# Value slabs ahead of query and key slabs at the head of a fused two-block kernel

## The reference

```python
h = rmsnorm(x, norm_mix)                 # x: 512 tokens x 1024
p = h @ w_in                             # retention: q, k, v, g of 512 columns each, then 1824 for RWKV-7
q, k = rope(q, positions), rope(k, positions) * 64 ** -0.5
s = (q_i . k_j) * gamma_h ** (i - j)     # i >= j, for each head h
y = s @ v                                # computed here over all 512 tokens at once
```

## Time and profile before

| | us |
|---|---|
| median of three runs | 1325.1 |
| lowest and highest | 1322.62, 1326.82 |
| the profiled execution's own time | 1322.79 |
| its span, first to last instruction | 1320.9 |
| mean granted TensorE clock in it | 0.989 |

### The profile page before, as it was taken

One profiled execution on the slowest core, in us unless ns is written; L12 is line 12 of the kernel. 1 busy time (PEld: TensorE's weight loads), 2 busy tenths in 40 slices (PEclk: granted clock), 3 DMA queues, 4 the chain that ended last, 5 costly groups with the idle time before them and its releaser, 6 DMA issues.

```text
span 1320.9 us, 20739 instructions
## 1 busy us (share of the span) xinstructions
PE 1262.7 (96%) x8308; PEld 1003.9 (76%) x8308; DVE 708.3 (54%) x827; ACT 542.7 (41%) x730; POOL 533.6 (40%) x245
## 2 busy tenths in 40 slices
PE   5999999888899999999999999999999999999995
PEld 3777757677787877788888888888776777777873
DVE  8888756757568532336224143144477755442833
ACT  5332253244343443543222132235342469885342
POOL 4442222710157732364444444446433322223453
PEclk9999999989999999999999999999999999999998
DMA  6571111110054221223222222222422321112221
GB/s 226 156 227 64 64 48 59 54 35 4 4 179 156 96 80 48 64 83 99 102 99 97 96 96 96 96 96 97 152 80 80 114 70 65 64 65 67 99 90 64
DMA packets 35098, 119.91 MB, mean 91 GB/s; under 512 B 4544, under 2 KB 4672, under 8 KB 34624
## 3 DMA queue, kind: packets, MB, share of 16 engines
q1 hardware_dynamic: 29808, 105.78, 23.7%
q10 hardware_dynamic: 5200, 12.85, 3.1%
HBM read 111.01 MB, written 2.10 MB: 86 GB/s over the span
## 4 chain that ended last, share of the span: by engine, by line
PE 79%; DVE 13%; ACT 4%; issue 2%; ACTq 1%; DMA 1%; POOL 0%; DVEq 0%; SPq 0%
PE banks L1381 20%; PE banks L1383 20%; PE banks L1382 20%; DVE y_mid L829 2%; PE banks L1402 1%; PE banks L1403 1%; PE banks L1404 1%; DVE tmp L829 1%; PE banks L1844 1%; PE banks L1860 1%; PE banks L1949 1%; DVE a_lo L837 1%; DVE qk L829 1%; PE banks L1934 1%; DVE x_res L837 1%
## 5 line engine op out<-in xcount | busy, mean ns | idle before, releaser
L338 POOL TENSOR_TENSOR w_lo<-w_raw,w_hi 128x1024 fp32r<-128x1024 f32 x145 | 353.7, 2440 | 537.7 <-ACT w_hi L401 537.4
L401 ACT ACTIVATE w_hi<-w_raw 128x1024 fp32r<-128x1024 f32 x145 | 153.8, 1061 | 333.1 <-PE banks L1383 213.2
L1381 PE MATMUL banks<-a_hi,w_hi 128*128 128x512 f32 x584 | 235.3, 403 | 14.2 <-DVE a_lo L837 12.2
L1383 PE MATMUL banks<-a_hi,w_lo 128*128 128x512 f32 x616 | 241.0, 391 | 0.0
L1382 PE MATMUL banks<-a_lo,w_hi 128*128 128x512 f32 x584 | 228.6, 391 | 0.0
L1383 PE MATMUL banks<-b_hi,w_lo 128*128 128x512 f32 x384 | 149.5, 389 | 0.0
L1381 PEld LDWEIGHTS banks<-a_hi,w_hi 128*128 128x128 f32 x584 | 110.0, 188 | 48.9 <-issue 16.9
L1383 PEld LDWEIGHTS banks<-a_hi,w_lo 128*128 128x128 f32 x616 | 116.2, 189 | 24.9
L829 DVE TENSOR_TENSOR x_res<-banks,x_res 128x512 f32<-128x512 f32 x56 | 38.7, 691 | 178.7 <-PE banks L1383 178.5
L338 POOL TENSOR_TENSOR w_lo<-w_raw,w_hi_mlp 128x1024 fp32r<-128x1024 f32 x36 | 87.2, 2423 | 106.4 <-ACT w_hi_mlp L401 106.4
L1382 PEld LDWEIGHTS banks<-a_lo,w_hi 128*128 128x128 f32 x584 | 110.4, 189 | 21.6 <-issue 0.7
(11 more groups left out here) (369 smaller groups left out, 2381.9 us busy)
## 6 DMA issues: line engine op xcount, KB each, us to landing
w_raw<-in_weights SPq DMA_DIRECT2D x189, 512.0 KB, 3.2
x_in<-in_x SPq DMA_DIRECT2D x4, 512.0 KB, 6.4
rot<-qk ACTq DMA_DIRECT2D x32, 64.0 KB, 2.0
decay<-in_decay ACTq DMA_DIRECT2D x1, 2048.0 KB, 9.7
x_res<-in_x ACTq DMA_DIRECT2D x4, 512.0 KB, 5.6
out_fm<-x_res SPq DMA_DIRECT2D x8, 256.0 KB, 2.1
consts<-in_consts SPq DMA_DIRECT2D x1, 1209.0 KB, 12.1
q_twice<-q_twice ACTq DMA_DIRECT2D x8, 128.0 KB, 3.2
```

The costliest lines, as they stand in the source:

```text
L338: nc.gpsimd.tensor_tensor(o, a, b, op).then_inc(S(name), 1)
L401: return nc.scalar.activation(o, a, f, **kw)
L1381: mm(o, high[:, w], hi[:, kc, :], start=kc == first, stop=False)
L1383: done = mm(o, w_lo[:, s % 4, w], hi[:, kc, :], start=False, stop=kc == last)
```

## The change

- Value slabs are 0 to 3; query and key slabs are 4 to 11, in the order query tile 0, key tile 0, query tile 1, key tile 1 and so on (`head_tile`). The weight layout follows.
- Value slab s starts with `a_lo` of its two x tiles. It is summed into banks 2 to 5; the values are scaled by VectorE in the second round, behind the rope of the first tile.
- ScalarE squares all eight x tiles, after the splits of slabs 0, 1 and 2; VectorE sums them; one matmul (two passes) with ones follows slab 2. GpSimd makes no squares.
- The slab 1 split comes after the fourth `a_hi`; SP loads weight slab 1 ahead of x tiles 4 to 7.
- ScalarE issues the loads of `w0` and `decay` behind the sum of squares, before the root; earlier they were issued at slab 8.
- The angle's last three VectorE operations come ahead of the reciprocal, and the cosine right behind it.
- Slab 12 follows the last key slab at once, so `rope(7)` and the `ret_lo` of the last three tiles come behind the masks of heads 0, 1 and 2. A pair of heads waits only for its own two tiles (`q_stacked0` to `q_stacked3`).
- `rot` moves from the place of `s_ret` to that of `kr`.

```diff
-S_RQ, S_RK, S_RV = 0, 4, 8
+S_RV, S_QK = 0, 4
-S_RET = S_RV + 4
+S_RET = S_QK + 8
+        def qk_taken(i):
+            return i + 1 if i < 2 else S_QK + i + 1
+        def head_tile(i):
+            return i // 2 + NF * (i % 2)
...
-                if s == 0:
-                    for i in range(4):
-                        load_x(i)
+                if s < 2:
+                    load_x(2 * s)
+                    load_x(2 * s + 1)
...
             for kc in range(KC):
                 x_hi(kc)
-            split_hi(1)
-            for kc in range(N_POOL_SQ, KC):
+                if kc == 3:
+                    split_hi(1)
+            split_hi(2)
+            for kc in range(KC):
                 x_squares(kc)
...
-                split_hi(s + 2)
+                if s > 0:
+                    split_hi(s + 2)
+                if s == 2:
+                    act.wait_ge(S("ssq_done"), 1)
+                    act.dma_start(w0[:], ins["w0"]).then_inc(S("decay_loaded"), 16)
+                    act.dma_start(decay[:], ins["decay"]).then_inc(S("decay_loaded"), 16)
+                    actv(rstd[:], psum[7][:], sqrt, bias=C("eps6"), scale=1.0 / DM).then_inc(A("rms_ready"), 1)
...
+                    if i == 1:
                         dve.wait_ge(S("column_done"), 1)
+                        cp(r_tok[:], psum[6][:, 0:8]).then_inc(D("column_ready"), 1)
+                        for t in range(TT):
+                            ts(v_ret[:, t, :], psum[2 + t][:], r_tok[:, 2 * t:2 * t + 1], None, ALU.mult).then_inc(D("tile_taken"), 1)
...
                 if S_RET <= s < S_RET + RH:
                     masked_scores(s - S_RET)
+                if s == S_WA:
+                    rope(7)
+                if S_WA <= s < S_WA + 3:
+                    ret_lo(s - S_WA + 5)
...
+                if s == 2:
+                    pe.wait_ge(S("x_sq_sum"), KC - 1)
+                    mm(psum[7][:], C("ones"), sq_in[:, 0, :], start=True, stop=True).then_inc(S("ssq_done"), 1)
+                if s == S_QK:
+                    pe.wait_ge(S("rstd_ready"), 1)
                     for t in range(TT):
+                        last = mm(psum[6][:, 2 * t:2 * t + 2], rstd[0:1, t * P:(t + 1) * P], C("ones", 0, 2)[0:1, :],
...
+                    if h % 2 == 0:
+                        pe.wait_ge(S("q_lo_ready"), 2 * h + 4)
+                        pe.wait_ge(S(f"q_stacked{h // 2}"), 4 * 16)
                     if h == 0:
-                        pe.wait_ge(S("q_lo_ready"), 16)
-                        pe.wait_ge(S("q_stacked"), 16 * 16)
                         pe.wait_ge(S("tile_taken"), S_RET)
+                        pe.wait_ge(S("column_ready"), 1)
```

More of the change, by code:

```diff
@@ L443, in exps, with swap_halves, ret_hi @@
                 actv(e_exc[:, f, :], be[:], exp).then_inc(A("exps_ready"), 1)
[L445 to L449, removed]
+            def swap_halves(i):
+                j = head_tile(i)
+                act.wait_ge(S("tile_taken"), qk_taken(i))
+                if i >= 2:
+                    act.wait_ge(S("rope_done"), i - 1)
                 for r in range(0, P, HD // 2):
                     o = r ^ (HD // 2)
[L452 removed]
+                    act.dma_start(rot[o:o + HD // 2, i % 2, :], qk[r:r + HD // 2, j, :]).then_inc(S(f"rot_loaded{i % 2}"), 16)
             def ret_part(j, k):
                 return q_twice[k][:, j, :] if j < NF else k_stack[k][:, j - NF, :]
[L458 to L459 removed]
+            def ret_hi(i):
+                j = head_tile(i)
+                act.wait_ge(S("rope_done"), i + 1)
                 for k in range(2):
@@ L470, in ret_stack @@
                     src = ret_part(j, k)[r] if j < NF else qk_lo[r, j, :]
-                    act.dma_start(ret_part(j, k)[other].bitcast(F32), src.bitcast(F32)).then_inc(S("q_stacked"), 16)
+                    act.dma_start(ret_part(j, k)[other].bitcast(F32), src.bitcast(F32)).then_inc(S(f"q_stacked{i // 2}"), 16)
             def silu(f):
@@ L485, in _ @@
                     actv(trig[:, 1, :], trig[:, 0, :], ACT.Sin, scale=0.5).then_inc(A("sines_ready"), 1)
[L486 to L494, removed]
+                i = s - S_QK
+                if 0 <= i < 8:
+                    swap_halves(i)
+                if 3 <= i < 11:
+                    ret_hi(i - 3)
+                if 4 <= i < 12:
+                    ret_stack(i - 4)
                 if s > S_RG:
@@ L872, in _ @@
                 x_lo(kc)
-            for kc in range(N_POOL_SQ + 1, KC):
+            for kc in range(1, KC):
                 x_square_sum(kc)
@@ L946, in _ @@
             mixed = [(low, 0), (low, 1), (low, 2)] + [(d, f) for d in (kk, rx, vx) for f in range(NF)]
[L947 to L953, removed]
+            for s in range(S_QK, S_MK):
                 dve.wait_ge(S("slab_done"), s + 1)
                 bank = psum[s % 2]
[L956 to L971, removed]
@@ L972, in _ @@
+                i = s - S_QK
+                if i < 8:
+                    tt(qk[:, head_tile(i), :], bank[:], rstd[:], ALU.mult).then_inc(D("tile_taken"), 1)
+                    if i >= 1:
+                        rope(i - 1)
+                    if i >= 3:
+                        ret_lo(i - 3)
+                    if i == 1:
                         dve.wait_ge(S("column_done"), 1)
[L973 to L976, removed]
+                        cp(r_tok[:], psum[6][:, 0:8]).then_inc(D("column_ready"), 1)
+                        for t in range(TT):
+                            ts(v_ret[:, t, :], psum[2 + t][:], r_tok[:, 2 * t:2 * t + 1], None, ALU.mult).then_inc(D("tile_taken"), 1)
@@ L1361, in _ @@
             mm = nc.tensor.matmul
-            wide_slabs = set(range(S_RV, S_WA)) | set(range(S_MV, S_WOUT)) | set(range(S_VIN, S_V2))
+            wide_slabs = set(range(S_RV, S_QK)) | set(range(S_MV, S_WOUT)) | set(range(S_VIN, S_V2))
             def begin(s):
@@ L1370, in begin @@
                 if before >= 0:
-                    pe.wait_ge(S("tile_taken"), before + 1)
+                    pe.wait_ge(S("tile_taken"), qk_taken(before - S_QK))
             def part(s, hi, lo, kcs, ready=None, k=0, at=0, first=0, last=KC - 1):
@@ L1396, in wide @@
                 for i, kc in enumerate(kcs):
+                    if ready:
+                        pe.wait_ge(S(ready), kc + 1)
                     for t in range(hi.shape[2] // P):
@@ L1469, in _ @@
             for s in range(S_MK):
-                if S_RV <= s < S_WA:
-                    if s == S_RV:
-                        pe.wait_ge(S("column_ready"), 1)
+                if s < S_QK:
                     i = s - S_RV
-                    wide(s, a_hi, a_lo, (2 * i, 2 * i + 1), (4, 5, 6, 7))
+                    wide(s, a_hi, a_lo, (2 * i, 2 * i + 1), (2, 3, 4, 5), "a_lo_ready")
                 else:
[L1476 to L1483, removed]
+                    slab(s, a_hi, a_lo)
+                if s == 2:
[3 more added lines that the diff above has]
+                    pe.wait_ge(S("rstd_ready"), 1)
                     for t in range(TT):
-                        last = mm(psum[5][:, 2 * t:2 * t + 2], rstd[0:1, t * P:(t + 1) * P], C("ones", 0, 2)[0:1, :],
+                        last = mm(psum[6][:, 2 * t:2 * t + 2], rstd[0:1, t * P:(t + 1) * P], C("ones", 0, 2)[0:1, :],
                                   start=True, stop=True)
@@ L2089, in lay_out @@
     rw = 2048
-    s = slabs(w_in[:, 0:1024]) + wide(w_in[:, 1024:1536])
+    s = wide(w_in[:, 1024:1536]) + slabs(w_in[:, 0:1024].reshape(DM, 2, NF, P).transpose(0, 2, 1, 3).reshape(DM, 1024))
     s += slabs(w_in[:, rw + 1536:rw + 1792]) + slabs(np.concatenate([w_in[:, rw + 1792:], pad], axis=1))
```

49 lines of the change are left out of this document (22 added, 27 removed).

## The result

The changed kernel takes 1327.56 us, the median of 20 runs (1323.28 to 1328.99); the kernel before, run beside it, 1325.24 (20 runs, 1320.73 to 1326.82). The ratio is 1.0016 with a 95% interval of 1.0008 to 1.0023: some 2 us slower, which is within the 0.3% that was called no change. The forecast was 1325.6 us, with a range of 1318.5 to 1329.5 that holds the result. The profiled execution took 1325.93 us, with a span of 1324.1 and a mean granted clock of 0.991.

A forecast was written before the change was run, and what follows sets the result against it. TensorE, busy 96% of the span, was taken as the bound. 6.9 gained, 4.9 lost waiting and 2.5 lost to the clock gave -0.5 us: forecast median 1325.6 us, range 1318.5 to 1329.5.

The forecast's parts named there:

- gain of 6.9 us: Up to the end of slab 12: 6.9 - 1.1 + 0.5 + 0.6 = 6.9 us gained.
- wait of 4.9: Behind slab 12: VectorE's backlog makes the first mask late, a loss of 4.9 us, bounds 4.2 and 5.9.
- clock loss of 2.5: Behind the wait for the first mask: TensorE's clock falls to 1.2 GHz, loss 2.5 us, bounds 0 and 2.9.
- the 4 to 6.5: Sign that the forecast is right: TensorE waits 4 to 6.5 us for `s_ret` near 94 to 100 us.
- First stretch: Value slabs in front: slab 1 starts at 17.7 us in place of 24.6, gain 6.9 us.
- waiting for the squares: After slab 2: the matmuls of the squares wait 0.5 us, part of a cost of 1.1 us.
- rival 3: Norm's chain late: TensorE waits 2 to 4 us before slab 5; time 1327.6 to 1329.6 us; chance 0.15.
- that is absorbed by the fifth round: Query and key rounds: four value tiles add 3.1 us of VectorE to the second round, absorbed by the fifth.
- Second hold: Behind slab 12: GpSimd's subtraction can hold VectorE's copy of `spread_r`, which then takes 1.7 us more.
- rival 2: Clock stays up: idle under 4.3 us with the copy first, 2.7 us gained, 1322.4 us; chance 0.15.
- Rival 1: No VectorE backlog: the mask is in time, no clock falls, 1318.2 to 1320.2 us; chance 0.25.
- carried along: Past 200 us: the change edits only one semaphore's count, so a time won earlier stays won.

The follow-up runs named there:

- e3_v_first: Changed kernel with the four value tiles scaled in the first query round, not the second; ratio 0.9994 to the kernel before.
- e1_again: Changed kernel run again with no edit; ratio 1.0014 to the kernel before.
- e4_act_order: Changed kernel with ScalarE's copies of a round put ahead of that round's rotation transfers; ratio 1.0016 to the kernel before.
- e2_fill: Changed kernel with dummy matmuls, nine ahead of slab 11 and twelve ahead of the scores of head 1; ratio 1.0020 to the kernel before.
- e5_clock: e3_v_first with 26 dummy matmuls in its only wait, ahead of the scores of head 1; ratio 0.9987 to the kernel before.
- e10_decay_late: Changed kernel with the loads of w0 and decay issued at slab 8 again; ratio 1.0014 to the kernel before.
- e6_spread_late: e3_v_first with VectorE's copy of spread_r moved three slabs later; ratio 0.9974 to the kernel before.
- e7_mask_first: e3_v_first with the spread_r copy three slabs later and each mask right behind shift, ahead of the mix's other operations; ratio 0.9965 to the kernel before.

## Why the prediction was right

**The sum held, in part by luck.** It had a gain of 6.9 us, a wait of 4.9 and a clock loss of 2.5: half a microsecond later. The mark is 0.55 us later. The kinds of loss were right, a late first mask and a clock that falls behind it. But four terms were off, and their errors cancelled: 1.6 us more was won up to slab 5, 2.6 us of waits came before slab 12 where the sum had a gain of 0.6, the wait for `s_ret` was 3.5 us, below the 4 to 6.5 that the prediction named as its sign, and the clock cost 0.7 us more.

**First stretch: right.** Up to slab 5 the sum was 6.9 - 1.1 + 0.5 = 6.3 us; measured 7.9. The clock rose 2.8 us sooner than in the profile of before, which is 1.4 of it. e3_v_first, with a rise at 14.8, starts slab 5 at 41.90: 6.8 us ahead. Of the 0.5 us of waiting for the squares 0.3 came: the last matmul of slab 2 starts at 27.30, the sums end at 27.78 and are used at 27.83. The norm's chain (rival 3) was in time with 2.6 us to spare: the reciprocal ends at 37.20, slab 4 at 39.8.

**The step that failed: "that is absorbed by the fifth round".** I put the value tiles into the second round at no cost beyond VectorE's time. But the third round's tile then comes 3 us late, its rotation issues with it (55.83), and VectorE stands idle for 3.92 us until they land. A subtraction held for 2.0 us follows (65.31). The tile of slab 8 starts 6.1 us after its slab ends (62.85), not about 2.5. So 0.4, 0.7 and 2.7 us of TensorE's waits and a first fall of the clock came before slabs 9 to 11, where I had 0.6 us, and the wait for `s_ret` was 3.5 us, below my 4.9. e3_v_first shows it: with the values one round earlier these three waits are gone and the one behind slab 12 is 6.4 us. The first mask starts at 98.82 us in after and at 96.88 in e3_v_first, with its copy held for 2 us: the step mostly moved where TensorE pays.

**Second hold: it comes in some profiles and not in others.** The copy of `spread_r` escaped in after by 0.6 us, and also in e1_again and e4_act_order (0.69 us each). It was held in e2_fill, e3_v_first, e5_clock and e10_decay_late (2.66 to 2.73 us). Moving it in e6_spread_late won 2.8 us of waiting: the whole held copy, 2.66 us, and not only my 1.7 for the hold.

**The clock: right in kind, mis-sized.** Falls came as forecast behind the long waits, and also behind one of 2.70 us; rival 2 is refuted. One costs about 1.6 us (e5_clock), not 2.5; but there were two of them. The length of a wait alone does not tell whether the clock falls: in e4_act_order it did after one of 1.84 us (0.64 and 0.80 from 78 to 84 us), in e10_decay_late it stayed at 1.00 after one of 2.32, in e7_mask_first after one of 2.12. The Trainium skill (TensorE: Matmul & The Clock Gate, "Why this matters for your kernels") speaks of gaps of more than about 3 us; here 2.70 us was enough, and the measurement decides.

**Rival 1 is refuted too.** VectorE's backlog was there; only with what stood ahead of the mask taken away (e7_mask_first) does the change give what this rival promised, and only at the mark: its time of 1318.2 to 1320.2 was not reached (1321.63).

**The ledger.** From slab 5 to the mark: -7.9 at its start, +3.8 in the waits before slabs 9 to 11 less 1.2 of before's, +3.0 more for `s_ret`, +3.2 for two falls: +0.9 us, against 0.55 measured.

**A time won early is not simply carried along.** The prediction took that for granted. GpSimd's subtractions let one follow it. Near 260 us (259.45 in before) after is still 0.55 us behind and e7_mask_first 6.45 ahead. At 373.24 us it is 2.75 behind and 1.4 ahead, at 407.37 it is 3.3 behind and 0.7 ahead, and so it stays to the end of the spans (1324.1 and 1320.1 against 1320.9). All of the difference arises between 260 and 410 us, where the changes edit nothing. The clock falls there two to five times, and not in the same way in two executions. The length from the mark to the end was 1164.7 to 1167.4 us in the five profiles with a mark before 158, and 1161.6 to 1165.3 in the seven with one from 159 on. So an early mark goes with a longer stretch behind it; why was not tried.

**What stays open.** The medians differ by 2.3 us and the marks by 0.55. The rise of the clock explains part: over the eleven profiles of changed kernels in the table it lies at 14.3 us on average, so after's 12.8 was early by 1.5, and a mark of about 160.5 is typical, 1.3 us behind before's. The rest lies in the stretch past the mark, which differs even between two profiles of one kernel: the `mem_k` row comes 211.3 us behind the mark in after and 208.6 in e1_again (209.1 in before, 213.4 in e7_mask_first).

## What to carry to other kernels

If slack slabs between a producer's rounds and its first consumer are taken away, write down all that stands ahead of the consumer's first operation in its queue, and put that operation first: here three small operations ahead of a mask, one or two of them held, cost more than the whole reordering lost. Extra work goes into a round in which its engine is idle; one round later it delayed transfers, and these delayed the rounds behind it. Filling TensorE's idle time can keep the clock up (1.3 to 1.6 us in e5_clock), but it does not hasten the engine that is waited for. And follow a gain to the end of the kernel: of 6.4 us won at the mark 3.9 to 4.6 were left.

## What the runs showed of the hardware that was not expected

- The time at which the clock rises after the start of work differed between executions from 12.5 to 16.2 us, with work starting at 9.5 to 10.2 in all of them. It shifts a kernel whose first slabs are never starved by half of that (slab 5 starts at 40.79 us in after with a rise at 12.8, at 42.08 in e5_clock with 15.4).
- A wait of TensorE of 2.70 us was followed by a stretch at 0.50, one of 1.84 us (e4_act_order) by stretches at 0.64 and 0.80, but one of 2.32 us (e10_decay_late) by none below 1.00. Some falls ended sooner than others: in after the clock is back at 1.00 in the second stretch of 3 us, in e2_fill it is at 0.50 for two and at 0.87 in the third.
- Whether VectorE's copy of `spread_r` took 0.69 or 2.7 us went with which of the two engines started first, the copy (by 0.6 to 1.4 us) or GpSimd's subtraction (by 0.2 to 0.4 us); it went one way in three profiles and the other way in four.
- Four rotation issues took 2.44 us of ScalarE's queue in most rounds of after and 3.73 us in one (55.83 us), and VectorE waited 3.9 us for them.
